# A hybrid convolution decoder layer in split fp32: normalising 256 tokens first, per token, and loading the residual a second time

## The reference, cut to what matters

```python
h = _rmsnorm(x, g_mix)
z = jnp.einsum("btd,de->bte", h, w_in)
a_val, a_gate, b_B, b_C, b_x, g_A, g_B = jnp.split(z, splits, axis=-1)
u = a_val * jax.nn.sigmoid(a_gate)
v, new_a = _causal_dwconv(u, buf_a, conv_a_w)          # 31 taps
v = _layernorm(v + conv_a_b, ln_a_g, ln_a_b)
y_a = jnp.einsum("btc,cd->btd", jax.nn.silu(v), w_a_out)
q, new_b = _causal_dwconv(b_C * b_x, buf_b, conv_b_w)  # 3 taps
y_b = jnp.einsum("btc,cd->btd", b_B * q, w_b_out)
merged = jax.nn.sigmoid(g_A) * y_a + jax.nn.sigmoid(g_B) * y_b
x = x + jnp.einsum("btd,de->bte", merged, w_o)
h2 = _rmsnorm(x, g_ffn)
f_gate, f_up = jnp.split(jnp.einsum("btd,df->btf", h2, w_up), [D_FF], axis=-1)
f_conv, new_f = _causal_dwconv(f_gate, buf_f, conv_f_w)
x = x + jnp.einsum("btf,fd->btd", jax.nn.silu(f_conv) * f_up, w_down)
```

## Time and profile before

| | us |
|---|---|
| median of 3 runs (873.62 to 1047.33) | 874.61 |
| the profiled execution | 874.33 |
| its span | 872.5 |
| PE busy in it | 862.6 (99%) |
| DVE busy | 598.4 (69%) |
| ACT busy | 347.4 (40%) |
| POOL busy | 117.3 (13%) |

### The profile page before, as it was taken

One profiled execution on the slowest core, in us unless ns is written; L12 is line 12 of the kernel. 1 busy time (PEld: TensorE's weight loads), 2 busy tenths in 40 slices (PEclk: granted clock), 3 DMA queues, 4 the chain that ended last, 5 costly groups with the idle time before them and its releaser, 6 DMA issues.

```text
span 872.5 us, 19208 instructions
## 1 busy us (share of the span) xinstructions
PE 862.6 (99%) x7174; PEld 860.5 (99%) x7174; DVE 598.4 (69%) x903; ACT 347.4 (40%) x578; POOL 117.3 (13%) x84
## 2 busy tenths in 40 slices
PE   8999999999999999999999999999999999999997
PEld 8999999999999999999999999999999999999996
DVE  6899999999999966665555766666666665333233
ACT  7663646364332335752234532333223233322222
POOL 2283837484000000000000000000000000000000
PEclk9999999999999999999999999999999999999999
DMA  6624233433333332333223243223223323332212
GB/s 205 170 74 120 75 96 96 143 96 98 105 98 97 93 109 76 97 96 97 83 87 96 76 119 96 82 87 96 84 84 96 96 66 94 89 98 81 87 46 99
DMA packets 157461, 84.70 MB, mean 97 GB/s; under 512 B 3078, under 2 KB 155964, under 8 KB 157396
## 3 DMA queue, kind: packets, MB, share of 16 engines
q1 hardware_dynamic: 154545, 82.32, 32.0%
q10 hardware_dynamic: 2875, 1.82, 0.7%
HBM read 81.70 MB, written 3.51 MB: 98 GB/s over the span
## 4 chain that ended last, share of the span: by engine, by line
PE 98%; DVE 1%; POOL 0%; issue 0%; ACT 0%; DVEq 0%; ACTq 0%; POOLq 0%
PE psum L1141 62%; PE psum L1147 32%; PE psum L1334 1%; PE psum L1123 1%; PE psum L1346 1%; DVE tmp L747 0%; POOL act L343 0%; PE psum L1298 0%; PE psum L1114 0%; PE psum L1228 0%; PE psum L1206 0%; PE psum L1106 0%; DVE act L754 0%; ACT act L401 0%; DVE y L1075 0%
## 5 line engine op out<-in xcount | busy, mean ns | idle before, releaser
L1141 PE MATMUL psum<-act,w_hi 128*128 128x260 f32 x2664 | 349.8, 283 | 1.2 <-DVE act L754 0.9
L1141 PEld LDWEIGHTS psum<-act,w_hi 128*128 128x128 f32 x2664 | 330.8, 188 | 1.9 <-issue 1.1
L700 DVE TENSOR_TENSOR w_lo<-raw,w_hi 128x1024 fp32r<-128x1024 f32 (+2 forms) x156 | 188.5, 1210 | 92.3 <-ACT w_hi L365 91.8
L1141 PE MATMUL psum<-mid,w_hi 128*128 128x260 f32 x1920 | 249.3, 282 | 0.0
L1141 PEld LDWEIGHTS psum<-mid,w_hi 128*128 128x128 f32 x1920 | 238.1, 188 | 0.0
L365 ACT ACTIVATE w_hi<-raw 128x1024 fp32r<-128x1024 f32 (+2 forms) x156 | 157.0, 1007 | 193.2 <-PE psum L1147 193.1
L1147 PE MATMUL psum<-act,w_lo 128*128 128x260 f32 x1332 | 189.2, 282 | 0.0
L1147 PEld LDWEIGHTS psum<-act,w_lo 128*128 128x128 f32 x1332 | 172.1, 188 | 0.0
L1147 PE MATMUL psum<-mid,w_lo 128*128 128x260 f32 x960 | 135.1, 283 | 0.0
L1147 PEld LDWEIGHTS psum<-mid,w_lo 128*128 128x128 f32 x960 | 123.4, 188 | 0.0
L350 POOL TENSOR_TENSOR gate_a<-gate_a,prods 128x512 f32<-128x512 f32 x72 | 110.1, 1529 | 74.1 <-ACT prods L418 65.7
(11 more groups left out here) (159 smaller groups left out, 444.5 us busy)
## 6 DMA issues: line engine op xcount, KB each, us to landing
raw<-in_w_in SPq DMA_DIRECT2D x56, 512.0 KB, 3.9
raw<-in_w_up SPq DMA_DIRECT2D x44, 512.0 KB, 3.8
raw<-in_w_down SPq DMA_DIRECT2D x16, 384.0 KB, 3.2
raw<-in_w_down SPq DMA_DIRECT2D x16, 320.0 KB, 3.0
raw<-in_w_b_out SPq DMA_DIRECT2D x8, 512.0 KB, 3.8
raw<-in_w_a_out SPq DMA_DIRECT2D x8, 512.0 KB, 3.7
raw<-in_w_o SPq DMA_DIRECT2D x8, 512.0 KB, 3.6
v<-in_x_prompt SPq DMA_DIRECT2D x4, 512.0 KB, 5.2
```

What stands on the lines that cost most here:

```text
L700: ve.tensor_tensor(w_lo[:, s, 0:k, :], raw[:, s, 0:k, :], w_hi[:, s, 0:k, :], ALU.subtract).then_inc(lo_done, 1)
L1141: pe.matmul(a[:, h, :], w_hi[:, s, j, :], rhs[:, 2 * k + part, h * H:(h + 1) * H], start=start and part == 0, stop=False)
```

## The change

**Head.** The prompt is worked off in two halves of 256 tokens (`HALF` = 0 to 255, and 256 to 519 with the samples). VectorE scales each token's row, where a token is a partition, by its inverse root (`row_scale`), and TensorE transposes the scaled rows; nothing is spread by a diagonal, and no `xT` is copied out for the prompt. Root and mean are one ScalarE instruction. With the transposed tokens still in PSUM, ScalarE writes hi (scaled by `g_mix`) from there and VectorE lo, in pieces of 256. TensorE does the hi passes and lo passes of units 0 and 1 for the first 256 tokens, then transposes tokens 256 to 511, then does the rest. GpSimd splits the lo of weight blocks 0 and 1. SP loads prompt tiles 2 and 3 behind weight blocks 0 and 1. There are 14 transposes of the identity in place of 32.

**Residual.** The x that `G_O` adds is loaded again, in four DMAs of 512 KB, each of 32 partitions, in runs of 32 floats (128 bytes); SP issues them between the loads of `w_a_out`, after a wait on `prod_done`. VectorE turns it, one instruction of 512 columns for each feature tile.

**All units.** A unit's two matmuls now have 256 and 264 tokens in place of 260 and 260. A result is 520 neighbouring columns over two banks (columns 256 to 775 of the pair).

The diff, cut:

```diff
+        Q = 32
         x_tok = [vf[:, t * D:(t + 1) * D] for t in range(TT)] + [ybf[0:B, D:2 * D]]
-        T_BANK = [4, 0, 2, 4, 2]
-        TOK = [(TT, B)] + [(t, P) for t in range(TT)]
+        x_sample_n = ybf[0:B, 2 * D:3 * D]
+        ORDER = (0, 2, 4, 6, 1, 3, 5, 7)
+        x_back = vf[:, 0:SEQ * KT].rearrange("p (j k c) -> p k j c", k=KT, c=Q)
...
+        HALF = ((0, 2 * P), (2 * P, N))
...
+            at = 2 * (s % 2) * BANK + BANK - 2 * P
+            return flat[:, at:at + N]
...
+                    for t in range(2, TT):
+                        load_tokens(t)
...
-            plain(G_AOUT, kview(w_a_out), 0)
+            for i in range(KT):
+                load(G_AOUT + i, i % RING, kview(w_a_out)[:, :, i * P:(i + 1) * P])
+                if RING - 1 <= i < RING - 1 + P // Q:
+                    a = i - (RING - 1)
+                    sp.wait_ge(prod_done, START + KT)
+                    sp.dma_start(vf[Q * a:Q * (a + 1), 0:SEQ * KT],
+                                 x_prompt[0].rearrange("t (k a c) -> a t k c", k=KT, c=Q)[a]).then_inc(x_again, 16)
...
-            for k in range(1, KT, 2):
-                pool.wait_ge(h_hi, k + 1)
-                pool.tensor_tensor(act[:, 2 * k + 1, :], h_tmp[k % 4], act[:, 2 * k, :], ALU.subtract).then_inc(h_lo_odd, 1)
+            for s in range(2):
+                pool.wait_ge(hi_done, s + 1)
+                pool.tensor_tensor(w_lo[:, s, :, :], raw[:, s, :, :], w_hi[:, s, :, :], ALU.subtract).then_inc(lo_done, 1)
...
-            for j, (t, n) in enumerate(TOK):
+            def square_root(j, t):
...
+                sc.wait_ge(x_squared, j + 1)
+                sc.activation(rs[0:n, t:t + 1], stat[0:n, 18 + t:19 + t], ACT.Sqrt, scale=1.0 / D, bias=ms[0:n, t:t + 1]).then_inc(x_root, 1)
+
+            def hi_half(s, part):
+
+                ks = slice(part * KT // 2, (part + 1) * KT // 2)
+                if part == 0:
+                    sc.wait_ge(raw_in[s], 16)
+                sc.activation(w_hi[:, s, ks, :], raw[:, s, ks, :], ACT.Copy).then_inc((w_half, hi_done)[part], 1)
+
+            def h_hi_split(h, at):
+
+                k = ORDER[at]
+                if at < 4:
+                    sc.wait_ge(half_turned, 4 * h + at + 1)
+                else:
+                    sc.wait_ge(h_lo, KT * h + at - 3)
+                sc.activation(act[:, 2 * k, h * 2 * P:(h + 1) * 2 * P], psum[:, 4 + k // 2, (k % 2) * 2 * P:(k % 2 + 1) * 2 * P],
+                              ACT.Copy, scale=gm[:, k:k + 1]).then_inc(h_hi, 1)
+
+            square_root(0, TT)
+            for t in range(2):
+                square_root(t + 1, t)
+            sc.wait_ge(gm_set, 1)
+            hi_half(0, 0)
+            for at in range(2):
+                h_hi_split(0, at)
+            hi_half(0, 1)
+            hi_half(1, 0)
+            for at in range(2, 4):
+                h_hi_split(0, at)
+            hi_half(1, 1)
+            for at in range(4, KT):
+                h_hi_split(0, at)
+            for t in range(2, TT):
+                square_root(t + 1, t)
+            sc.wait_ge(x_inv, TT + 1)
+            sc.activation(x_tok[TT - 1][:, D // 2:D], x_tok[TT - 1][:, D // 2:D], ACT.Copy, scale=rs[:, TT - 1:TT]).then_inc(x3_scaled, 1)
+            sc.wait_ge(sample_set, 1)
+            sc.activation(act_sample[:, 0], h_sample, ACT.Copy).then_inc(sample_hi, 1)
+            for at in range(KT):
+                h_hi_split(1, at)
+            for s in range(2, RING):
...
+            def row_inverse(j, t):
+                n = P if t < TT else B
...
+            def row_scale(t, part):
+                cols = slice(part * D // 2, (part + 1) * D // 2)
+                ve.tensor_scalar(x_tok[t][:, cols], x_tok[t][:, cols], rs[:, t:t + 1], None, ALU.mult).then_inc(x_scaled, 1)
+
+            def h_lo_split(h, at):
+                k = ORDER[at]
+                cols = slice(h * 2 * P, (h + 1) * 2 * P)
+                ve.wait_ge(h_hi, KT * h + at + 1)
+                ve.scalar_tensor_tensor(out=act[:, 2 * k + 1, cols], in0=psum[:, 4 + k // 2, (k % 2) * 2 * P:(k % 2 + 1) * 2 * P],
+                                        scalar=gm[:, k:k + 1], in1=act[:, 2 * k, cols], op0=ALU.mult,
+                                        op1=ALU.subtract).then_inc(h_lo, 1)
...
+            ve.wait_ge(sample_turned, 1)
+            ve.tensor_scalar(gm[:, :], psum[:, 1, KT * B:KT * B + KT], 1.0, None, ALU.mult).then_inc(gm_set, 1)
+            ve.tensor_scalar(xT[:, :, SEQ:N], psum[:, 1, 0:KT * B].rearrange("p (k b) -> p k b", k=KT), 1.0, None, ALU.mult).then_inc(gm_set, 1)
+            row_inverse(0, TT)
+            ve.tensor_scalar(x_sample_n, x_tok[TT], rs[0:B, TT:TT + 1], None, ALU.mult).then_inc(x_scaled, 1)
+            for t in range(2):
+                row_inverse(t + 1, t)
+                for part in range(2):
+                    row_scale(t, part)
+            ve.wait_ge(gm_set, 2)
+            for at in range(KT):
+                h_lo_split(0, at)
+            row_inverse(3, 2)
+            for part in range(2):
+                row_scale(2, part)
+            row_inverse(4, 3)
+            row_scale(3, 0)
+            ve.wait_ge(sample_turned, 2)
+            ve.tensor_tensor(h_sample, psum[:, 3, 0:KT * B].rearrange("p (k b) -> p k b", k=KT),
+                             gm[:, :].rearrange("p (k o) -> p k o", o=1).broadcast_to([P, KT, B]), ALU.mult).then_inc(sample_set, 1)
+            ve.wait_ge(sample_hi, 1)
+            ve.tensor_tensor(act_sample[:, 1], h_sample, act_sample[:, 0], ALU.subtract).then_inc(sample_lo, 1)
+            for at in range(KT):
+                h_lo_split(1, at)
...
+            ve.wait_ge(x_again, 16 * P // Q)
+            for i in range(KT):
+                g = G_O + i
+                ve.transpose(xT[:, i, 0:SEQ].rearrange("p (r j) -> p j r", r=Q), x_back[:, i]).then_inc(x_again_turned, 1)
+                out_of_psum(g, g)
+                ve.wait_ge(x_again_turned, i + 1)
...
-            warm(8, 7)
-            for j, (t, n) in enumerate(TOK):
...
-            warm(22, 0)
...
+            def turn_tokens(t, ks):
+                for k in ks:
+                    at = (k % 2) * 2 * P + (t % 2) * P
+                    last = pe.transpose(psum[:, 4 + k // 2, at:at + P], x_tok[t][:, k * P:(k + 1) * P], ident[:, :])
+                    if t % 2 == 1 and k % 2 == 1:
+                        last.then_inc(half_turned, 1)
...
+            warm(6)
+            pe.wait_ge(x_in[TT], 16)
+            turn_sample(x_tok[TT], 1)
+            pe.wait_ge(gm_in, 16)
+            pe.transpose(psum[:, 1, KT * B:KT * B + KT], gm_row, ident[0:KT, 0:KT]).then_inc(sample_turned, 1)
+            warm(8)
+            for t in range(2):
                 for part in range(2):
-                    for h in range(2):
-                        pe.matmul(a[:, h, :], w_hi[:, s, j, :], rhs[:, 2 * k + part, h * H:(h + 1) * H],
+                    pe.wait_ge(x_scaled, 2 + 2 * t + part)
+                    turn_tokens(t, range(part * KT // 2, (part + 1) * KT // 2))
...
+            def first_hi(s, h, at):
+
+                k = ORDER[at]
+                lo, hi = HALF[h]
+                if h == 0:
+                    pe.wait_ge(*((w_half, s + 1) if k < KT // 2 else (hi_done, s + 1)))
+                pe.wait_ge(h_hi, KT * h + at + 1)
+                pe.matmul(acc_half(s, h), w_hi[:, s, k, :], act[:, 2 * k, lo:hi], start=at == 0, stop=False)
+                pe.wait_ge(h_lo, KT * h + at + 1)
+                pe.matmul(acc_half(s, h), w_hi[:, s, k, :], act[:, 2 * k + 1, lo:hi], start=False, stop=False)
...
+                for first in (0, 2):
                     for s in range(2):
-                        if k == 0:
-                            pe.wait_ge(hi_done, s + 1)
-                        hi_pass(s, act, a[s], k, k, k == 0)
-                    if k == KT // 2 - 1:
-                        pe.wait_ge(xT_half, 2)
-                        pe.wait_ge(xT_done, TT + 1)
-                        pe.wait_ge(rows_in, 16 * 8)
-                        for j, n in enumerate(CROWS):
-                            last = pe.transpose(psum[:, 5, sum(CROWS[:j]):sum(CROWS[:j]) + n], crow[j][0:n, :], ident[0:n, 0:n])
-                        last.then_inc(cst_turned, 1)
+                        for at in range(first, first + 2):
+                            first_hi(s, 0, at)
+                for at in range(4, KT):
+                    for s in range(2):
+                        first_hi(s, 0, at)
                 for s in range(2):
-                    pe.wait_ge(lo_done, s + 1)
-                    for k in range(KT):
-                        last = lo_pass(s, act, a[s], k, k, k == KT - 1)
-                    last.then_inc(mm_done, 1)
+                    first_lo(s, 0)
+                for part in range(2):
+                    pe.wait_ge(x_scaled, 6 + part)
+                    turn_tokens(2, range(part * KT // 2, (part + 1) * KT // 2))
```

(34 more changed lines are left out.)

193 lines of the change are left out of this document (62 added, 131 removed).

## The result

The changed kernel takes **877.93 us** (median of 6 runs, 877.71 to 878.23), the kernel before 874.60 in its runs beside it: ratio 1.004, 95% interval [1.003, 1.005]. That is 3.3 us more. It is under 2%, inside the range of 872.0 to 880.5, and 2.9 us above the 875.0 forecast, which had foreseen 0.4 us of change. The profiled execution has a span of 875.6 us against 872.5.

What follows compares the result with a forecast made beforehand. TensorE bounds the kernel, busy 862.6 of 872.5 us and 98% of the chain. 874.33 - 1.0 (head) + 1.5 (widths), with second load and turns 0, gave 874.8, taken as 875.0 us; range 872.0 to 880.5.

Steps and rivals of the forecast that it cites:

- Head, -1.0: Start of the program up to unit 2: unit 2 starts at about 27.9 instead of 28.96, 1.0 us less.
- the eviction chain: ScalarE in the head: constants copied, table load, dummy, then unit 0's eviction, over at 27.8; late next, holding unit 2.
- GpSimd's splits: Head: two lo splits of 1024 columns, 2.1 to 4.1 us each, ending between 15 and 19; 0.5 us of wait taken.
- 256 and 264, +1.5: Matmuls of all units: new widths cost between 0 and +2.4 us over the program; +1.5 taken.
- steady units at 5.76 to 5.78 us: Sign to look for in the changed profile: steady units take this instead of 5.75 us; over 5.8 would mean wrong.
- Rival 3: All units: width costs nothing, 873.5 us, or 872.0 with the head's better end; chance 0.24.
- Second load, 0: Four new DMAs among the `w_a_out` loads: 3.3 us each, block 7 lands at 411.6, hidden by 8.7 us.
- Rival 1: Second load: small packets are slow and the queue becomes a wait; 0.14 for about 881 us, 0.04 for 909.
- point of decision: Second load: the small-packet rival decides the time from 21 ns a packet on, where the cover ends (5.5 us a DMA).
- VectorE's turns, 0: Eight turns of 512 columns for `G_O`: 0.48 to 1.5 us each, up to 1.2 us costs nothing; 0 taken.
- Rival 2: Head: TensorE starves and its clock falls or rises late; 878 us, chance 0.14.
- the prediction's own sign of it: Head: the prediction is wrong if transposes after 10 us still take 0.21 us each.

Runs made afterwards that it cites:

- a_260: The changed kernel with only the first two units cut 256 + 264, all others 260 + 260; 873.58 us, ratio 0.9990 to the kernel before.
- a_again64: The changed kernel with its second load of the tokens in 64-byte pieces instead of 128; 883.47 us, ratio 1.0099 to the kernel before.
- b_ or x_: Nine variants of the kernel before, results as 520 columns in a row, with various cuts (x_: second matmul reads overlapping tokens); 873.70 to 887.22 us.
- b_256: The kernel before with every unit cut 256 + 264 and results as 520 columns in a row; 878.63 us, ratio 1.0047.
- best: a_260 plus three more warming transposes and the Sigmoid table load issued ahead of the wait for the constants; 872.57 us, ratio 0.9978 to the kernel before.

## Why the prediction was right, and where it was not

The class, the range and the sign of each term held; one term was mis-sized, and with it the change as a whole: +3.3 us measured, +0.4 forecast.

- **Head, -1.0: right**, and nearly every step of it. Block 0's wait ended at 8.36 (foretold 8.5), the last lo of the first half at 14.74 (14.7), the hi passes at 15.58 (15.3), the last of tile 3 was turned at 20.13 (20.5), the eviction chain over at 27.89 (27.8), unit 2 began at 27.94 (27.9). It was named as late next, and moving the table load bears it out: 0.8 us more. That the sum met 1.0 to a tenth is in part luck: unit 2 starts at 27.6 in a_260 and at 29.5 in a_again64, whose heads are the same, and between 28.8 and 29.6 in the kernels named b_ or x_ (where the cut of units 0 and 1 has a part in it).
- **GpSimd's splits:** 2.4 us each, over at 15.82 where TensorE got to them at 15.58. The 0.5 us of wait that I took did not come: the first unit's is over long before.
- **256 and 264, +1.5: the step that failed.** It measured +4.0: after the start of unit 2 the changed kernel has 847.6 us of span and b_256 847.5, the kernel before 843.6 and a_260 843.7. The prediction bounded it by the last unit, +2.4, and by 0, with the reason that time is linear in the columns. The upper bound was none: that unit reads and writes in another order than the others, so its 0.35 ns a matmul was no ceiling. In the late stretch it was (5.787 - 5.753) / 48 = 0.7 ns. Taking 1.5 between the two then made it worse. The prediction's own sign, steady units at 5.76 to 5.78 us, was nearer: 0.01 to 0.03 us over some 140 units is up to 4.2 us, not 1.5. "Width" was also the wrong name: 252 + 268 costs nothing, 258 + 262 three times as much as 256 + 264. The price is that of particular cuts, and why is open.
- The Trainium skill ("TensorE: Matmul & The Clock Gate", section Back-to-back issue gap) gives the gap of a matmul by itself as columns at the granted rate plus a constant, and says that in a stream the weight loads enter too. By the formula 248 + 272, 252 + 268, 256 + 264 and 258 + 262 would all cost what 260 + 260 does. Of these only 252 + 268 did. Rival 3, which rested on the same linearity, would have been right for a cut four columns further on.
- **Second load, 0: right**, with less to spare than I said. Block 7's wait ended at 415.90 instead of 411.6, 5 us ahead of need instead of 8.7. A packet of 128 bytes had its 11 to 13 ns where nothing else was on the queue, which is 2.9 to 3.4 us a DMA. What the prediction left out is that SP's issues could stall and the queue stand empty, as around 406.5. Rival 1's slow packet is out, and its point of decision is real: a_again64 went over it. The Trainium skill ("DMA: Bandwidth & Descriptors", Specifications) gives 512 bytes as the least for full rate, and a read-modify-write below. The queue lines agree on the rate: a packet of 64 bytes takes 10.9 ns and one of 128 bytes 11 to 13, against the prediction's 27 for 512 bytes, so bytes move more slowly in small ones; a doubling of the 27 ns they do not show.
- **VectorE's turns, 0: right.** 1.07 us each, inside the 0.48 to 1.5 given, and under the 1.2 us of slack.
- **Rival 2, the clock in the head:** it did happen, and so did the prediction's own sign of it: the last transposes of tile 1, after 10 us, still stand 0.21 apart. The level rose at 13.0 us, 3.4 us later than before. The rival priced it at 3 us; it cost nothing that shows (a_260, at 12.2, loses nothing at the lo matmuls to `best`, at 8.8), since most of the matmuls at the lower level had to wait for their data anyway. Where the level stayed low until 15.6 (a_again64), it made 0.8 us. So the rival was sound, and its price a matter of how late the rise comes.
- The sum by what was measured: 872.5 - 1.0 + 4.0 = 875.5, and the span is 875.6.

## What to carry to other kernels

When TensorE is 98% of the chain, a head step and a change of shape are not of one kind: the first is paid once, the second in every matmul. 20 ns a unit is invisible in any one row and outweighed 1 us of careful head work. So when a kernel's tile is cut anew, keep the new cut where it buys something (here the first two units) and leave the steady ones as they are. And measure the pace by starts of units far apart, for each tile that is read, before and after; try a few cuts on the chip, since the nearest ones may be the worst.
